# In the last pair of heads the rounded half of a probability is copied by VectorE instead of exponentiated a second time on ScalarE

## The chip, the cores and the metric

The kernel runs on one core of a Trainium2 chip. The metric is the device time of one launch in microseconds (us); lower is better. Engines are written as in the profile: PE is TensorE, ACT is ScalarE, DVE is VectorE, POOL is GpSimd, SP is SyncE, whose queue issues the DMAs here.

## The reference

One step of a one-layer streaming encoder: an RMS norm, one input projection that feeds two groups of attention heads, an output projection, and a SwiGLU feed-forward layer. The change lies in group A, the forgetting attention: 8 heads of 64, causal, over 1024 prompt rows and over 32 sample rows with 256 cached ones. Cut to it:

```python
s = jnp.einsum('bqhd,bkhd->bhqk', qi, k).astype(jnp.float32) * ATTN_SCALE
s = s + (ci[..., None] - cT[:, :, None, :])      # running sums of log forget gates
s = jnp.where((kpos[None, :] <= qpos[:, None])[None, None], s, NEG_INF)
p = jax.nn.softmax(s, axis=-1)
return jnp.einsum('bhqk,bkhd->bqhd', p.astype(v.dtype), v)
...
h = h + mixed @ w_out                            # both groups, each RMS-normalised
```

All data is float32.

## The kernel before, in words

**Split products.** PE multiplies a rounded 32-bit type (fp32r) fast, and the kernel keeps float32 accuracy by splitting every operand x into a rounded first half (hi) and the rest (lo = x - hi). A product is three matmuls, hi*hi, hi*lo and lo*hi (lines L526 to L528 for most of them, L719 for scores). So every operand costs two evictions or copies besides its computation.

**Units.** The heads are worked in four pairs. A pair has 15 units, numbered v = 15*pair + j, v from 0 to 59; the last pair is v = 45 to 59. A unit is one block of 128 keys against up to 512 queries, for both heads h of the pair. Queries go in three chunks: j = 0 to 3 have 512, 384, 256 and 128 queries, j = 4 to 8 have 512, j = 9 to 11 have 384, 256 and 128, and j = 12 to 14 are the sample's 32 rows. For each unit:

- `fox_scores(v)`: PE writes the scores of both heads to two banks of PSUM (six matmuls L719, on masked units some L725, last two L731). In the last pair it has two sets of banks and waits only for the exponentials of v-2.
- `fox_exp(v)`: ACT takes the exponential of each head's scores twice, once into `ph_x` in fp32r (the hi half, L1129) and once into `sp_x` in float32 (L1130). The second raises the semaphore `x_e`.
- `fox_lo(v)`: POOL waits for `x_e` and writes `pl_x = sp_x - ph_x` (L1834), one instruction a head, and raises `x_pl`.
- `fox_values(v)`: PE waits for `x_pl` of both heads and adds six matmuls (L526 to L528) to the output banks; it raises `x_pv`. The buffers of `ph_x` and `sp_x` go by v % 2, so `fox_exp(v)` waits for `x_pv` of v-2.

**The order.** Each engine has one program, written out step by step. PE in step v does `fox_scores(v)`, then the minima, projections and small transposes that a schedule gives to this step, then `fox_values(v-1)`. So scores run one unit ahead of values. What else is in the last pair:

- The output weights. In steps v = 46 to 53 ACT ends its step with `out_weights_hi` (`wo_hi`, L963, 128x1024) and DVE ends its own with `split_lo` (`wo_lo = raw - wo_hi`, L1352, both inputs in SBUF).
- The end of a chunk. ACT copies the output banks to `ot_x` (`fox_out`, L1144), PE transposes them (L612), and DVE divides them by their row sums (reciprocal L1454, product `og_x` L1458), from where a DMA stores them. For chunk 0 this is in step 50, where PE has these transposes, one of a small tile (`amx`, L599) and then `fox_values(49)`.
- The minima. In steps 45 to 48 DVE finishes the row minima of this pair (L1510), and POOL splits them into `tm_x` (L1845, L1847).
- The hand-over. In step 59 ACT (behind `fox_exp(59)`) and DVE (at the start of its step) do `groups_norm(0)`, the norm of the first 128 rows of mixed heads (squares L1210, a square root L1213 with the load of its table, DVE L1365, L1369 and twice L1609). In step 60 ACT has `fox_out(59)`, in step 61 PE and DVE have chunk 2's transposes and divisions. PE then waits until all of these are done before it transposes the normed rows (`turn_mixed(0)`, L846) and goes on to the output projection and the feed-forward layer.

Of the kernel before, what the change touches and what calls it, by code (L numbers as in the profile page):

```python
# [10 lines left out]
ACT = mybir.ActivationFunctionType  # L11
# [12 lines left out]
PAIRS = NH // 2  # L24
# [65 lines left out]
FU = make_fox()  # L90
# [222 lines left out]
def build(nc, x_p, x_s, ck_fox, cv_fox, cl_fox, ck_swa, cv_swa, rel_bias, g_attn, w_in, b_forget, sinks,  # L313
# [15 lines left out]
    with ExitStack() as ctx:  # L329
# [128 lines left out]
        def bank_view(b, m, start, *dims):  # L458
# [5 lines left out]
            f_mm f_ev f_t f_chain f_act f_bt f_c c_out c_in band_ps band_sb band_out band_in bias_ready  # L464
            st0 st1 st_misc
            w_s w_add w_e w_pl w_m w_ttr w_tm w_es w_pv w_ot w_den og_w0 og_w1
            x_s x_e x_pl x_m x_ttr x_tm x_pv x_ot x_den x_og ones
            o_in0 o_in1 o_in2 o_in3 o_in4 o_in5 o_in6 o_in7 o_in8
            c_xin0 c_xin1 c_sq1 c_ms1 c_rt1 c_ri1 c_xn1 c_t1 c_hi1 c_lo1 c_k c_op c_h2 c_sq2 c_ms2 c_rt2 c_ri2
            c_xn2 c_t2 c_t3 c_hi3 c_lo3  # L470
# [487 lines left out]
        def _(act):  # L958
# [161 lines left out]
            def fox_exp(v):  # L1120
                i, j = v // NFU, v % NFU
                _, vb, _, rows, _, n, _, _, _ = FU[j]
                if v >= 2:
                    act.wait_ge(S["x_pv"], 2 * (v - 1))
                b = score_bank(v)
                for h in range(2):
                    act.wait_ge(S["x_s"], 2 * v + h + 1)
                    decay = negc[0:rows, vb, 2 * i + h:2 * i + h + 1]
                    act.activation(ph_x[2 * (v % 2) + h][0:rows, 0:n], ps[0:rows, b + h, 0:n], ACT.Exp, bias=decay, scale=-1.0)  # L1129
                    act.activation(sp_x[2 * (v % 2) + h][0:rows, 0:n], ps[0:rows, b + h, 0:n], ACT.Exp, bias=decay, scale=-1.0)\  # L1130
                       .then_inc(S["x_e"], 1)

# [216 lines left out]
        def _(dve):  # L1349
# [143 lines left out]
            def fox_minima(i, g):  # L1493
# [9 lines left out]
                for h in range(2):  # L1503
# [4 lines left out]
                    if chained:  # L1508
                        dve.wait_ge(S["x_ttr"], 2 * (at - 1) + h + 1)
                    dve.tensor_tensor_reduce(s, s, cb[0:m, h, k0:k0 + nk], 1.0, part if chained else 3.0e38,  # L1510
                                             ALU.add, ALU.min, final if last else part).then_inc(S["x_ttr"], 1)

            def items(*place):

                for kind, a in plan(*place):
                    if kind == "task":
                        task(*a)
                    elif kind == "mw":
                        window_minima(*a)
# [93 lines left out]
            for v in range(-LEAD, NX + 2):  # L1613
                if v == NX - 1:
                    groups_norm(0)
                for part in range(5):
                    items("x", v, part)
                if 0 <= v - OUT_SPLITS < KB:
                    k = v - OUT_SPLITS
                    split_lo(SPLIT_OUT + k, raw2d[k % 3], wo_hi[:, k, :], wo_lo[:, k, :])  # L1620
# [111 lines left out]
        def _(pool):  # L1732
# [96 lines left out]
            def fox_lo(v):  # L1829
                _, _, _, rows, _, n, _, _, _ = FU[v % NFU]  # L1830
                for h in range(2):
                    pool.wait_ge(S["x_e"], 2 * v + h + 1)
                    at = 2 * (v % 2) + h
                    pool.tensor_tensor(pl_x[at][0:rows, 0:n], sp_x[at][0:rows, 0:n], ph_x[at][0:rows, 0:n].bitcast(F32),  # L1834
                                       ALU.subtract).then_inc(S["x_pl"], 1)
# [319 lines left out]
```

## Time and profile before

| | |
|---|---|
| median of 3 runs | 1499.74 us (1499.39 to 1500.48) |
| the profiled execution | 1497.76 us, span 1496.0 us |
| PE busy | 1410.3 us, 94% of the span |
| DVE, ACT, POOL busy | 579.4, 477.5 and 214.1 us |
| granted clock of PE, mean over the span | 0.976 |
| last pair, exponentials of v = 45 to 59 | 510.46 to 564.33 us from the span's start |

Times in rows are in us from the span's start. The table's shares are averages over stages with different limits; the last pair of heads is some 54 us of the span, and from 578 us on PE is busy without a gap. A row's "x2" merges two instructions that follow each other, its duration then reaches from the first's start to the second's end; what stands in brackets is the engine's idle time before it and what ended it.

### The profile page before, as it was taken

The numbers are of one execution on the slowest core, as the hardware profiler recorded it, in microseconds if no ns is written. First come the engines' busy times: TensorE is split into PE (matmuls) and PEld (weight loads), VectorE is DVE, ScalarE is ACT, GpSimd is POOL, SyncE is SP. The second block draws the span as 40 slices with busy tenths as digits, with TensorE's granted clock in tenths as the row PEclk, the third lists the DMA queues.
The fourth block names the chain that finished last, engine by engine and source line by source line (L and its number), as shares of the span: only waits on it lengthen the run. The fifth ranks groups of instructions, "written<-read, shape, count | busy, mean of one in ns | idle before, by whom it ended". The sixth has DMA issues, their size and how long they took to land.

```text
span 1496.0 us, 22497 instructions
## 1 busy us (share of the span) xinstructions
PE 1410.3 (94%) x9041; PEld 1303.2 (87%) x9041; DVE 579.4 (39%) x1374; ACT 477.5 (32%) x1044; POOL 214.1 (14%) x317
## 2 busy tenths in 40 slices
PE   5989987999999887999999999999999999999996
PEld 3878876877888756887999999999999999999996
DVE  6235542323232334444325242433333342425155
ACT  6336552354545473433321212021211112111103
POOL 2125542253524250000000000000000000000000
PEclk9999999999999898999999999999999999999998
DMA  7621113111212043112221111111111202020002
GB/s 193 111 60 30 34 44 98 44 47 41 90 41 73 23 135 124 43 40 64 85 79 38 54 43 43 43 43 43 43 43 42 61 25 71 15 73 30 12 1 116
DMA packets 104687, 87.34 MB, mean 58 GB/s; under 512 B 14336, under 2 KB 95328, under 8 KB 104072
## 3 DMA queue, kind: packets, MB, share of 16 engines
q1 hardware_dynamic: 104584, 85.91, 19.9%
q8 instruction: 72, 1.18, 0.3%
q14 instruction: 31, 0.25, 0.1%
HBM read 71.10 MB, written 14.89 MB: 57 GB/s over the span
## 4 chain that ended last, share of the span: by engine, by line
PE 87%; DVE 4%; ACT 3%; issue 3%; DMA 2%; POOL 1%; SPq 0%; DVEq 0%; ACTq 0%
PE ps L526 27%; PE ps L527 25%; PE ps L528 25%; PE ps L719 2%; PE ps L846 2%; DVE ps L1476 1%; PE ps L685 1%; DMA out<-outb 1%; PE ps L647 1%; DMA out<-raw 1%; PE ps L731 1%; PE ps L605 1%; ACT sp_x L1130 1%; ACT ph_x L1129 1%; DVE sp_w L1488 1%
## 5 line engine op out<-in xcount | busy, mean ns | idle before, releaser
L1682 DVE TENSOR_TENSOR outs<-outs,ps 128x384 f32<-128x384 f32 (+1 forms) x264 | 134.6, 510 | 108.7 <-PE ps L528 108.7
L1667 DVE TENSOR_TENSOR gu<-ps,sg 128x384 f32<-128x384 f32 (+1 forms) x66 | 34.6, 525 | 238.1 <-PE ps L528 238.1
L1834 POOL TENSOR_TENSOR pl_x<-sp_x,ph_x 128x512 fp32r<-128x512 f32 (+5 forms) x120 | 102.2, 866 | 149.4 <-ACT sp_x L1130 147.8
L1295 ACT ACTIVATE h_hi<-gu 128x384 fp32r<-128x384 f32 (+1 forms) x66 | 32.9, 498 | 222.7 <-DVE gu L1667 222.7
L1129 ACT ACTIVATE ph_x<-ps,negc 128x512 fp32r<-128x512 f32 (+5 forms) x120 | 63.1, 526 | 83.9 <-PE ps L731 83.9
L526 PE MATMUL ps<-f_hi,ff0hi 128*128 128x384 f32 (+1 forms) x264 | 85.7, 325 | 0.0
L526 PE MATMUL ps<-f_hi,ff3hi 128*128 128x384 f32 (+1 forms) x264 | 85.6, 324 | 0.0
L526 PE MATMUL ps<-f_hi,ff1hi 128*128 128x384 f32 (+1 forms) x264 | 85.6, 324 | 0.0
L526 PE MATMUL ps<-f_hi,ff2hi 128*128 128x384 f32 (+1 forms) x264 | 85.6, 324 | 0.0
L1289 ACT ACTIVATE sg<-ps 128x384 f32<-128x384 f32 (+1 forms) x66 | 30.5, 465 | 171.7 <-PE ps L528 171.7
L527 PE MATMUL ps<-f_lo,ff0hi 128*128 128x384 f32 (+1 forms) x264 | 85.2, 323 | 0.0
L527 PE MATMUL ps<-f_lo,ff1hi 128*128 128x384 f32 (+1 forms) x264 | 85.2, 323 | 0.0
L527 PE MATMUL ps<-f_lo,ff2hi 128*128 128x384 f32 (+1 forms) x264 | 85.2, 323 | 0.0
L527 PE MATMUL ps<-f_lo,ff3hi 128*128 128x384 f32 (+1 forms) x264 | 85.2, 323 | 0.0
L528 PE MATMUL ps<-f_hi,ff0lo 128*128 128x384 f32 (+1 forms) x264 | 85.1, 322 | 0.0
L528 PE MATMUL ps<-f_hi,ff1lo 128*128 128x384 f32 (+1 forms) x264 | 85.1, 322 | 0.0
L528 PE MATMUL ps<-f_hi,ff2lo 128*128 128x384 f32 (+1 forms) x264 | 85.1, 322 | 0.0
L528 PE MATMUL ps<-f_hi,ff3lo 128*128 128x384 f32 (+1 forms) x264 | 85.1, 322 | 0.0
L526 PE MATMUL ps<-h_hi,ff4hi 128*128 128x384 f32 (+1 forms) x240 | 82.1, 342 | 0.6 <-DVE outs L1686 0.5
L526 PE MATMUL ps<-h_hi,ff5hi 128*128 128x384 f32 (+1 forms) x240 | 78.3, 326 | 0.0
L527 PE MATMUL ps<-h_lo,ff5hi 128*128 128x384 f32 (+1 forms) x240 | 77.5, 323 | 0.0
L527 PE MATMUL ps<-h_lo,ff4hi 128*128 128x384 f32 (+1 forms) x240 | 77.4, 322 | 0.0
(290 smaller groups left out, 3799.5 us busy)
## 6 DMA issues: line engine op xcount, KB each, us to landing
raw<-in_w_gate SPq DMA_DIRECT2D x22, 512.0 KB, 5.2
raw<-in_w_up SPq DMA_DIRECT2D x22, 512.0 KB, 5.0
raw<-in_w_down SPq DMA_DIRECT2D x22, 512.0 KB, 4.0
raw<-in_w_in SPq DMA_DIRECT2D x14, 512.0 KB, 3.9
cb<-c_scratch SPq DMA_DIRECT2D x4, 1312.0 KB, 6.6
xt<-in_x_prompt SPq DMA_DIRECT2D x8, 512.0 KB, 4.3
out<-outb SPq DMA_DIRECT2D x16, 256.0 KB, 2.4
raw<-in_w_out SPq DMA_DIRECT2D x8, 512.0 KB, 3.5
```

The costliest lines, as they stand in the source:

```text
L526: pe.matmul(out, wh, xh, start=start, stop=False)
L527: pe.matmul(out, wh, xl, start=False, stop=False)
L528: return pe.matmul(out, wl, xh, start=False, stop=stop)
L605: mm = pe.transpose(ps[0:m, b, (2 * kv + x) * P:(2 * kv + x + 1) * P], ot_w[kv][:, x * m:(x + 1) * m], ident[:])
L719: pe.matmul(ps[0:rows, b + h, 0:n], keys[i % 2][hs, k0:k0 + rows], queries[i % 2][hs, q], start=(part == 0), stop=False)
L846: mm = pe.transpose(ps[:, banks[j], k * m:(k + 1) * m], src[0:m, (4 * j + k) * P:(4 * j + k + 1) * P], ident[0:m, 0:m])
L1129: act.activation(ph_x[2 * (v % 2) + h][0:rows, 0:n], ps[0:rows, b + h, 0:n], ACT.Exp, bias=decay, scale=-1.0)
L1289: act.activation(sg[c][:, 0:n], bank(c, n), ACT.Silu).then_inc(S["g_sg"], 1)
L1295: act.activation(h_hi[par][:, f, c0:c0 + n], gu[(f + c) % 2][:, 0:n], ACT.Copy).then_inc(S["g_hi"], 1)
L1667: dve.tensor_tensor(gu[(f + c) % 2][:, 0:n], bank(3 + c, n), sg[c][:, 0:n], ALU.mult)\
L1682: add = dve.tensor_tensor(y, y, bank(6 + o % 2, whole * P).rearrange("p (t m) -> p t m", t=whole), ALU.add)
L1834: pool.tensor_tensor(pl_x[at][0:rows, 0:n], sp_x[at][0:rows, 0:n], ph_x[at][0:rows, 0:n].bitcast(F32), ALU.subtract).then_inc(S["x_pl"], 1)
```

## The change

In the last pair (i = 3, v = 45 to 59) ACT makes one exponential a head, into `sp_x`. DVE copies it to `ph_x`, which rounds it, in a new function `fox_round(v)`, behind part 1 of its step v. POOL's `fox_lo(v)` waits there for the copies (`x_r`) instead of the exponentials. `fox_round(v)` waits for the same `x_pv` as `fox_exp(v)`. PE's and SP's programs stay as they are.

```diff
                 for h in range(2):
                     act.wait_ge(S["x_s"], 2 * v + h + 1)
                     decay = negc[0:rows, vb, 2 * i + h:2 * i + h + 1]
-                    act.activation(ph_x[2 * (v % 2) + h][0:rows, 0:n], ps[0:rows, b + h, 0:n], ACT.Exp, bias=decay, scale=-1.0)
+                    if i < PAIRS - 1:
+                        act.activation(ph_x[2 * (v % 2) + h][0:rows, 0:n], ps[0:rows, b + h, 0:n], ACT.Exp, bias=decay, scale=-1.0)
                     act.activation(sp_x[2 * (v % 2) + h][0:rows, 0:n], ps[0:rows, b + h, 0:n], ACT.Exp, bias=decay, scale=-1.0)\
                        .then_inc(S["x_e"], 1)
...
+            def fox_round(v):
+
+                _, _, _, rows, _, n, _, _, _ = FU[v % NFU]
+                dve.wait_ge(S["x_pv"], 2 * (v - 1))
+                for h in range(2):
+                    at = 2 * (v % 2) + h
+                    dve.wait_ge(S["x_e"], 2 * v + h + 1)
+                    dve.tensor_copy(ph_x[at][0:rows, 0:n], sp_x[at][0:rows, 0:n]).then_inc(S["x_r"], 1)
...
                 for part in range(5):
                     items("x", v, part)
+                    if part == 1 and NX - NFU <= v < NX:
+                        fox_round(v)
                 if 0 <= v - OUT_SPLITS < KB:
                     k = v - OUT_SPLITS
                     split_lo(SPLIT_OUT + k, raw2d[k % 3], wo_hi[:, k, :], wo_lo[:, k, :])
...
                 for h in range(2):
-                    pool.wait_ge(S["x_e"], 2 * v + h + 1)
+                    if v < NX - NFU:
+                        pool.wait_ge(S["x_e"], 2 * v + h + 1)
+                    else:
+                        pool.wait_ge(S["x_r"], 2 * (v - NX + NFU) + h + 1)
                     at = 2 * (v % 2) + h
                     pool.tensor_tensor(pl_x[at][0:rows, 0:n], sp_x[at][0:rows, 0:n], ph_x[at][0:rows, 0:n].bitcast(F32),
                                        ALU.subtract).then_inc(S["x_pl"], 1)
```

Below, lines of the changed kernel are one higher on ACT and up to ten higher on DVE than the same lines before. DVE's program in steps 48 to 52 was this before: the weights' lower halves of the steps 48 and 49, in step 50 the two divisions of chunk 0, and a weight's half in each of the steps 50, 51 and 52.

```order
L1352 TENSOR_TENSOR wo_lo<-raw_62,wo_hi 128x1024
L1352 TENSOR_TENSOR wo_lo<-raw_60,wo_hi 128x1024
L1454 RECIPROCAL small<-ps 128x4
L1458 TENSOR_TENSOR og_x<-ps,small 128x4x64
L1454 RECIPROCAL small<-ps 128x4
L1458 TENSOR_TENSOR og_x<-ps,small 128x4x64
L1352 TENSOR_TENSOR wo_lo<-raw_61,wo_hi 128x1024
L1352 TENSOR_TENSOR wo_lo<-raw_62,wo_hi 128x1024
L1352 TENSOR_TENSOR wo_lo<-raw_60,wo_hi 128x1024
```

Of the changed kernel the same place, up to the copies of step 51:

```order
L1353 TENSOR_TENSOR wo_lo<-raw_62,wo_hi 128x1024
L1521 CAST ph_x_101<-sp_x_156 128x512
L1521 CAST ph_x_158<-sp_x_157 128x512
L1353 TENSOR_TENSOR wo_lo<-raw_60,wo_hi 128x1024
L1521 CAST ph_x_99<-sp_x_154 128x512
L1521 CAST ph_x_100<-sp_x_155 128x512
L1455 RECIPROCAL small<-ps 128x4
L1459 TENSOR_TENSOR og_x<-ps,small 128x4x64
L1455 RECIPROCAL small<-ps 128x4
L1459 TENSOR_TENSOR og_x<-ps,small 128x4x64
L1353 TENSOR_TENSOR wo_lo<-raw_61,wo_hi 128x1024
L1521 CAST ph_x_101<-sp_x_156 128x512
```

Two copies (`ph_x_101` and `ph_x_158` for odd units, `ph_x_99` and `ph_x_100` for even ones) now stand between any two weight halves, and in step 50 ahead of the divisions.

The end of DVE's last pair was this before: the divisions of chunk 1, `groups_norm(0)`, and the divisions of chunk 2.

```order
L1454 RECIPROCAL small<-ps 128x4
L1458 TENSOR_TENSOR og_x<-ps,small 128x4x64
L1365 TENSOR_SCALAR small<-small 128x2
L1369 RECIPROCAL small<-small 128x2
L1609 SCALAR_TENSOR_TENSOR raw_61<-oq,small,gains 128x512 x2
L1454 RECIPROCAL small<-ps 32x1
L1458 TENSOR_TENSOR og_x<-ps,small 32x64
```

Of the changed kernel the same place:

```order
L1455 RECIPROCAL small<-ps 128x4
L1459 TENSOR_TENSOR og_x<-ps,small 128x4x64
L1366 TENSOR_SCALAR small<-small 128x2
L1370 RECIPROCAL small<-small 128x2
L1619 SCALAR_TENSOR_TENSOR raw_61<-oq,small,gains 128x512 x2
L1521 CAST ph_x_101<-sp_x_156 32x32
L1521 CAST ph_x_158<-sp_x_157 32x32
L1455 RECIPROCAL small<-ps 32x1
L1459 TENSOR_TENSOR og_x<-ps,small 32x64
```

The copies of unit 59 stand behind the whole of `groups_norm(0)`, since DVE does that at the start of step 59.

ACT's program in steps 51 and 52 was this before, one unit of four exponentials and a weight's upper half, and the start of the next:

```order
L1129 ACTIVATE ph_x_101<-ps,negc 128x512
L1130 ACTIVATE sp_x_156<-ps,negc 128x512
L1129 ACTIVATE ph_x_158<-ps,negc 128x512
L1130 ACTIVATE sp_x_157<-ps,negc 128x512
L963 ACTIVATE wo_hi<-raw_62 128x1024
L1129 ACTIVATE ph_x_99<-ps,negc 128x512
```

and is this in the changed kernel:

```order
L1131 ACTIVATE sp_x_156<-ps,negc 128x512
L1131 ACTIVATE sp_x_157<-ps,negc 128x512
L963 ACTIVATE wo_hi<-raw_62 128x1024
L1131 ACTIVATE sp_x_154<-ps,negc 128x512
L1131 ACTIVATE sp_x_155<-ps,negc 128x512
```

Each unit has two instructions fewer in front of its weight's upper half.

## Rows read from the trace of the kernel before

**Rows 1.** Busy time by stretch: bounds, length, then PE, PEld, DVE, ACT, POOL, clock, DMA.

```profile
531.00:539.00 8.00, 4.57 (x32) 3.19 (x29) 3.58 (x6) 8.00 (x15) 4.01 (x4) 1.00 0.36 114
539.00:554.00 15.00, 12.86 (x67) 7.99 (x66) 6.14 (x4) 12.03 (x20) 9.19 (x8) 0.89 0.64 224
578.00:704.00 126.00, 126.00 (x662) 103.61 (x661) 60.29 (x109) 48.22 (x115) 0.00 (x0) 0.99 0.16 51
```

**Rows 2.** Timeline of PE in steps 51 to 54: values (L526) and scores (L719).

```profile
540.07 0.79 PE L719 MATMUL ps<-q_hi,k_hi 64*128 64x512 f32 x2
...
546.15 0.50 PE L526 MATMUL ps<-ph_x,vw_hi 128*128 128x512 f32 x1 [0.85 <-POOL pl_x L1834]
...
547.74 0.50 PE L719 MATMUL ps<-q_hi,k_hi 64*128 64x512 f32 x2
...
549.62 0.50 PE L526 MATMUL ps<-ph_x,vw_hi 128*128 128x512 f32 x1 [0.50 <-POOL pl_x L1834]
...
553.14 0.50 PE L526 MATMUL ps<-ph_x,vw_hi 128*128 128x512 f32 x1 [0.78 <-POOL pl_x L1834]
```

**Rows 3.** Timeline of ACT in the same steps.

```profile
542.24 0.69 ACT L1129 ACTIVATE ph_x<-ps,negc 128x512 fp32r<-128x512 f32 x1 [2.63 <-PE ps L731]
...
544.53 1.07 ACT L963 ACTIVATE wo_hi<-raw 128x1024 fp32r<-128x1024 f32 x1
...
549.21 0.69 ACT L1129 ACTIVATE ph_x<-ps,negc 128x512 fp32r<-128x512 f32 x1 [0.35 <-PE ps L731]
```

**Rows 4.** Timeline of POOL, units 49, 51, 52 and, first head alone, 54.

```profile
533.26 2.50 POOL L1834 TENSOR_TENSOR pl_x<-sp_x,ph_x 128x512 fp32r<-128x512 f32 x2 [2.31 <-ACT sp_x L1130]
...
543.58 2.52 POOL L1834 TENSOR_TENSOR pl_x<-sp_x,ph_x 128x512 fp32r<-128x512 f32 x2 [3.56 <-ACT sp_x L1130]
546.84 2.73 POOL L1834 TENSOR_TENSOR pl_x<-sp_x,ph_x 128x512 fp32r<-128x512 f32 x2 [0.74 <-ACT sp_x L1130]
...
553.61 1.44 POOL L1834 TENSOR_TENSOR pl_x<-sp_x,ph_x 128x384 fp32r<-128x384 f32 x1 [0.52 <-ACT sp_x L1130]
```

**Rows 5.** Timeline of DVE: three of the eight lower halves of output weights.

```profile
545.64 1.54 DVE L1352 TENSOR_TENSOR wo_lo<-raw,wo_hi 128x1024 fp32r<-128x1024 f32 x1 [4.54 <-ACT wo_hi L963]
548.90 1.75 DVE L1352 TENSOR_TENSOR wo_lo<-raw,wo_hi 128x1024 fp32r<-128x1024 f32 x1 [1.72 <-ACT wo_hi L963]
552.61 1.56 DVE L1352 TENSOR_TENSOR wo_lo<-raw,wo_hi 128x1024 fp32r<-128x1024 f32 x1 [1.97 <-ACT wo_hi L963]
```

**Rows 6.** Timeline of DVE: the instructions nearest to the new copy.

```profile
514.07 0.69 DVE L1416 TENSOR_TENSOR vw_lo<-ps,vw_hi 128x512 fp32r<-128x512 f32 x1 [2.15 <-ACT vw_hi L1079]
...
565.73 0.17 DVE L1365 TENSOR_SCALAR small<-small 128x2 f32<-128x2 f32 x1 [2.36 <-ACT raw L1210]
```

**Rows 7.** Timeline of DVE and PE around step 50, the end of chunk 0.

```profile
536.29 1.23 DVE L1352 TENSOR_TENSOR wo_lo<-raw,wo_hi 128x1024 fp32r<-128x1024 f32 x1 [3.00 <-ACT wo_hi L963]
...
538.12 0.24 PE L599 MATMUL ps<-ident,tm_x 32*128 32x32 f32 x1 [2.04 <-DVE og_x L1458]
```

**Rows 8.** Timeline of all engines over steps 59 to 61 and the hand-over.

```profile
563.54 0.28 ACT L1129 ACTIVATE ph_x<-ps,negc 32x32 fp32r<-32x32 f32 x1 [1.18 <-PE ps L731]
...
564.07 0.58 POOL L1834 TENSOR_TENSOR pl_x<-sp_x,ph_x 32x32 fp32r<-32x32 f32 x2 [1.38 <-ACT sp_x L1130]
...
564.71 0.28 PE L526 MATMUL ps<-ph_x,vw_hi 32*128 32x32 f32 x1 [0.49 <-POOL pl_x L1834]
...
565.28 0.26 PE L528 MATMUL ps<-ph_x,vw_lo 32*128 32x32 f32 x1
...
567.12 0.27 ACT L1144 ACTIVATE ot_x<-ps 128x32 f32<-128x32 f32 x2
...
567.44 1.42 DVE L1609 SCALAR_TENSOR_TENSOR raw<-oq,small,gains 128x512 f32<-128x512 f32 x2
...
569.46 0.21 DVE L1458 TENSOR_TENSOR og_x<-ps,small 32x64 f32<-32x64 f32 x1
569.99 1.94 PE L846 MATMUL ps<-ident,raw 128*128 128x128 f32 x8 [1.96 <-DVE og_x L1458]
```

More of the change, by code:

```diff
@@ L466, in build @@
             w_s w_add w_e w_pl w_m w_ttr w_tm w_es w_pv w_ot w_den og_w0 og_w1
-            x_s x_e x_pl x_m x_ttr x_tm x_pv x_ot x_den x_og ones
+            x_s x_e x_pl x_m x_ttr x_tm x_pv x_ot x_den x_og x_r ones
             o_in0 o_in1 o_in2 o_in3 o_in4 o_in5 o_in6 o_in7 o_in8
```

## Prediction

> **What bounds the kernel now.** I read the busy time by stretch first. From 578 us on PE has no gap [rows 1], so whatever delays the hand-over at the end of the last pair stays in the total. Inside the pair it is not so: of 531 to 539 us PE works 4.57 of 8.00 while ACT is busy for all of it, and of 539 to 554 PE works 12.86 of 15.00. Then I read PE's timeline for what ends those gaps. Each `fox_values` starts on POOL's `pl_x` after 0.50 to 0.85 us of waiting [rows 2]. So in the large units the bound is a loop through four engines. For unit 51, ACT starts at 542.24 [rows 3], POOL 1.34 later, at 543.58, and runs 2.52, to 546.10 [rows 4]; PE starts values(51) at 546.15. They last until scores(53) at 547.74, 1.59 later [rows 2], and ACT starts unit 53 at 549.21, 1.47 after that [rows 3]. Sum of the loop: 3.91 + 1.59 + 1.47 = 6.97 us, and values(51) to values(53) is 6.99. It carries every second unit, so a unit takes 3.5 us. Only what lengthens 3.91 counts, and half of it for each unit.
>
> **What the trace shows of DVE against POOL.** A weight's lower half takes 1.23 us alone, at 536.29 [rows 7]. The one asked at 545.64 ends at 547.18, 1.08 after POOL's 546.10. The one asked at 548.90 ends at 550.65, 1.08 after POOL's end at 546.84 + 2.73 = 549.57. It works the other way round as well: POOL begins the first head of unit 54 at 553.61 and ends it at 555.05, while DVE holds on to 552.61 + 1.56 = 554.17; the 0.88 behind that is all that 384 elements need [rows 4, 5]. So a DVE instruction with two inputs in SBUF and a POOL instruction exclude each other, and the later one waits in full. Before the change this is nearly free: `wo_lo` is asked when ACT's `wo_hi` ends, 544.53 + 1.07, near the end of POOL's second head, and it clears out before POOL's next unit, but for some 0.2 to 0.5. The Trainium skill, page "SBUF — State Buffer", section "Who interferes with whom", states this as a rule: the two share a port pair under an exclusive lock, whichever issued first. By that rule, the trace agrees, to the 1.08.
>
> **The change part by part.** ACT loses two exponentials a unit, 0.57 each in the large units (544.53 - 542.24 = 2.29 for four [rows 3]). DVE gains two copies. The trace has no copy from SBUF to SBUF on DVE. Its bounds are 0.17 (an instruction on two elements) and 0.69 (512 elements at one a cycle, from PSUM and SBUF [rows 6]); I take 0.69, the row with the copy's own size, and show what the other end does. The Trainium skill, page "VectorE: DVE Perf Modes", section "The perf-mode tier table", gives fp32 copies within SBUF twice that rate, an estimate of 0.42 for 512; its SBUF page adds that such a copy takes the port pair too.
>
> *Step a, the chain of a large unit (51).* From T, ACT's start. Now: first exponential, 0.69 and a hand-over of 0.08, then copy 0.69 and 0.08, so POOL starts at T + 1.54 in place of T + 1.34. Its first head ends at T + 2.79. By then the second copy is done, but ACT's `wo_hi` ends at T + 1.14 + 1.07 = T + 2.2, so DVE asks for `wo_lo` at about T + 2.3, in the middle of POOL's first head, no longer at the end of its second. It is next: T + 2.79 to T + 3.87. POOL's second head follows, to T + 5.12, and values start at T + 5.2. That is 1.3 more than 3.91. If POOL keeps its turn for the second head, `wo_lo` runs from T + 4.04 to T + 5.12, the next unit's first copy, wanted at T + 3.5 + 0.77 = T + 4.27, waits 0.85, and the loss is about 1.0 instead. With a copy of 0.42 that also excludes POOL, the second copy can't run under POOL's first head; it and `wo_lo` go between the heads (0.30 + 1.13 after POOL's first head at T + 1.27 to T + 2.52), and the end is again at T + 5.2. The three orders agree within 0.3.
>
> *Step b, units 52 and 53.* Now the turn-taking itself sets the pace: one copy 0.69 (nothing of this unit runs beside it), POOL 1.25, `wo_lo` 1.08, POOL 1.25, and some 0.15 of hand-overs, 4.4 us a unit against 3.5. Two units, 2 x 0.9 = 1.8. With the short copy the sum is 0.30 + 1.25 + 0.30 + 1.13 + 1.25 + 0.15, the same 4.4. Units 54 to 58 have no weights behind them; there a copy replaces an exponential in the chain, within 0.1 each either way, taken as 0.
>
> *Step c, step 50.* Before, DVE does its `wo_lo` at 536.29, then the divisions, and PE starts the small transpose at 538.12, with values(49) right behind it [rows 7]. The two copies of unit 50 now stand ahead of the divisions: 2 x 0.69 = 1.4. POOL's unit 49, which began at 533.26 [rows 4], starts behind its copies some 1.1 later, so its second head ends near where `wo_lo` begins, or after it: 1.1 more for one of them. Against it ACT, which never rests here [rows 1], reaches `wo_hi` 2 x 0.57 = 1.1 earlier. Sum +1.4; bounds 0.3 (short copies) and 2.0 (all of it in a row).
>
> *Step d, steps 45 to 48.* Their units are small or their weight halves far from POOL's work; PE waits there for evictions and minima. ACT's saved 1.1 at unit 45 advances the first eviction by about 0.3, and the copies in step 47 push POOL's `tm_x` back by more than that. This is inside the bounds of step c, which was counted from the present times.
>
> *Step e, the hand-over.* In E, ACT's start of unit 59, 563.54 before. ACT begins the squares 0.34 earlier, so `groups_norm(0)` ends on DVE at 567.44 + 1.42 - 0.34, E + 4.98 [rows 8]. Only then come the copies of unit 59, whose values so far ran under the load of the table. Now in a row: copy 0.17, POOL 0.08 + 0.58, PE 0.06 + 0.83 (564.71 to 565.54), ACT 0.1 + 0.27, transposes 0.3, divisions of the second head 0.4, and 0.3 to the start of L846 (569.67 to 569.99). E + 4.98 + 3.1 = E + 8.1; before it was E + 6.45. That is +1.6, and with PE's small matmuls slower after a rest of 4 us I take +1.9 (1.6 to 2.4). No work covers it: all engines wait for the same chain. SP's stores and loads behind `x_pv` and `og_x` shift with it and keep their lead over PE.
>
> **Sum.** 1.3 + 1.8 + 1.4 + 1.9 = 6.4 us. The profiled execution took 1497.76, which gives 1504.2; the median lies 1.98 above it, so I forecast 1499.74 + 6.4 = 1506.1. Bounds: 0.7 + 1.2 + 0.3 + 1.6 = 3.8 and 1.5 + 2.2 + 2.0 + 2.4 = 8.1, so 1503.5 to 1507.8 in this case.
>
> **Rivals.** *The copies slip between.* If POOL's two heads stay together and `wo_lo` ends before the next copy is due, steps a to c come to nothing, since a copy takes the place of an exponential of about its own length; step e stays. 1499.74 + 1.9 = 1501.6. Against it: `wo_lo` and both heads need 1.08 + 2.5, more than the 3.5 of a unit, already. *The clock falls.* PE's rests grow from 0.5 to 0.85 to some 1.5 us a unit. In 539 to 554 us the mean granted clock is 0.89 [rows 1], and scores(51), at 540.07 after the gap of step 50, took 0.79 for their first two matmuls instead of 0.50 [rows 2]. At the lower level, 1.2 GHz, values and scores of a large unit take some 1.2 more; for two more units 2.5, so 1508.6. *ScalarE's relief decides* (the other side). ACT is busy for the whole of 531 to 539. If its queue is the bound there and in 542 to 552, where `wo_hi` ends just as the next unit is due, 1.1 are saved at each of two units and 0.3 at unit 45; with short copies another 0.15 for each of three units. That is 3.0 off, against 1.9 of step e: 1498.6. It decides over step a as soon as `wo_lo` costs POOL less than 0.3 a unit; to be faster by over 0.2% it would need 4.9 off.
>
> **How the numbers follow.** My forecast has 0.63, the clock 0.15, the slipping copies 0.15, ScalarE's relief 0.07. About 0.2%, 3.0 us, is what a measurement of this kernel can tell from no change. The forecast and the clock give slower, 0.78; I add 0.01 for mixtures. Both others lie within 3.0 us: 0.22, less 0.03 for a larger relief. So faster 0.03, same 0.18, slower 0.79. The range takes in the slipping copies' 1501.6 and the clock's 1508.6: 1501.4 to 1508.8.
>
> **What would show it.** `wo_lo` of steps 51 to 53 begins between POOL's two heads, which no longer follow each other without a gap. From ACT's start to PE's values, unit 51 takes 5.2 instead of 3.91, and values(51) to values(53) 8.7 instead of 6.99. L846 starts 8.1 to 8.9 after ACT's start of unit 59 instead of 6.45. I am wrong if POOL's heads stay together and the spacing stays at 7.0, or if the copies take under 0.3.

## The result and the profile after

The changed kernel takes 1506.86 us (median of 6 runs, 1504.33 to 1509.70), the kernel before 1500.11 us beside it (6 runs, 1498.55 to 1501.64). The ratio is 1.0045, 95% interval 1.0032 to 1.0058: slower by 6.75 us, where 6.4 was forecast.

| | before | after |
|---|---|---|
| the profiled execution | 1497.76 us, span 1496.0 | 1509.70 us, span 1507.9 |
| PE busy | 1410.3 us | 1416.0 us |
| DVE, ACT, POOL busy | 579.4, 477.5, 214.1 us | 591.5, 466.2, 217.8 us |
| mean granted clock | 0.976 | 0.966 |

The profiled execution is the slowest of its six and 11.9 us longer than the one of before. Of that, 3.77 us lie ahead of ACT's start of unit 45 (514.23 against 510.46), where the programs are equal (the mean clock of the first 100 us is 0.90 after and 0.97 before), and 0.3 behind the hand-over (from L846's start to the end it is 926.3 us after and 926.0 before). So the change is read between two marks, ACT's start of unit 45 and the start of L846: 67.35 us after, 59.53 before, 7.82 more. This is the timeline of all engines after, steps 49 to 53, as [rows 2] to [rows 5] and [rows 7] show them before (start, duration, engine, line, operation, what it waited for):

```profile
538.73 1.29 ACT L1131 ACTIVATE sp_x<-ps,negc 128x512 f32<-128x512 f32 x2
538.90 2.26 DVE L1353 TENSOR_TENSOR wo_lo<-raw,wo_hi 128x1024 fp32r<-128x1024 f32 x1 [1.18 <-ACT wo_hi L963]
541.09 0.75 DVE L1521 CAST ph_x<-sp_x 128x512 fp32r<-128x512 f32 x2
541.76 0.17 DVE L1455 RECIPROCAL small<-ps 128x4 f32<-128x4 f32 x1
...
542.44 0.31 PE L599 MATMUL ps<-ident,tm_x 32*128 32x32 f32 x1 [3.75 <-DVE og_x L1459]
542.68 0.80 PE L526 MATMUL ps<-ph_x,vw_hi 128*128 128x512 f32 x1
...
547.71 1.27 ACT L1131 ACTIVATE sp_x<-ps,negc 128x512 f32<-128x512 f32 x2 [3.78 <-PE ps L731]
548.50 2.08 DVE L1521 CAST ph_x<-sp_x 128x512 fp32r<-128x512 f32 x2 [3.21 <-ACT sp_x L1131]
548.87 1.06 ACT L963 ACTIVATE wo_hi<-raw 128x1024 fp32r<-128x1024 f32 x1
549.01 1.29 POOL L1849 TENSOR_TENSOR pl_x<-sp_x,ph_x 128x512 fp32r<-128x512 f32 x1 [4.80 <-DVE ph_x L1521]
550.51 1.21 DVE L1353 TENSOR_TENSOR wo_lo<-raw,wo_hi 128x1024 fp32r<-128x1024 f32 x1
550.66 2.18 POOL L1849 TENSOR_TENSOR pl_x<-sp_x,ph_x 128x512 fp32r<-128x512 f32 x1 [0.36 <-DVE ph_x L1521]
551.64 1.82 DVE L1521 CAST ph_x<-sp_x 128x512 fp32r<-128x512 f32 x2
552.90 0.50 PE L526 MATMUL ps<-ph_x,vw_hi 128*128 128x512 f32 x1 [2.27 <-POOL pl_x L1849]
553.21 3.61 POOL L1849 TENSOR_TENSOR pl_x<-sp_x,ph_x 128x512 fp32r<-128x512 f32 x2 [0.36 <-DVE ph_x L1521]
553.39 2.31 DVE L1353 TENSOR_TENSOR wo_lo<-raw,wo_hi 128x1024 fp32r<-128x1024 f32 x1
...
556.72 0.43 DVE L1521 CAST ph_x<-sp_x 128x512 fp32r<-128x512 f32 x1 [1.03 <-ACT sp_x L1131]
556.87 0.50 PE L526 MATMUL ps<-ph_x,vw_hi 128*128 128x512 f32 x1 [1.03 <-POOL pl_x L1849]
...
561.07 0.50 PE L526 MATMUL ps<-ph_x,vw_hi 128*128 128x512 f32 x1 [1.47 <-POOL pl_x L1849]
```

A copy of 512 takes 0.43 alone (556.72) and two in a row 0.75 (541.09), not 0.69 apiece. In unit 51, though, the pair takes 2.08 (548.50): the first ends before POOL starts, at 549.01, and the second ends only 0.28 after POOL's first head, 550.58 against 550.30. Then `wo_lo` (550.51) goes, and POOL's second head needs 2.18 instead of 1.25. This is the order that step a gave for the short copy, and values(51) start 5.19 after ACT (552.90 - 547.71). The Trainium skill, page "VectorE: DVE Perf Modes", section "The perf-mode tier table", gives such copies two elements a cycle, and its page "SBUF — State Buffer", section "Who interferes with whom", says that they take the port pair in that mode. The trace agrees with both, to the 0.43 and the 550.58.

The hand-over after, as [rows 8]:

```profile
572.87 0.45 ACT L1131 ACTIVATE sp_x<-ps,negc 32x32 f32<-32x32 f32 x2 [3.10 <-PE ps L731]
...
576.44 1.41 DVE L1619 SCALAR_TENSOR_TENSOR raw<-oq,small,gains 128x512 f32<-128x512 f32 x2
577.77 0.25 DVE L1521 CAST ph_x<-sp_x 32x32 fp32r<-32x32 f32 x2
578.01 0.45 POOL L1849 TENSOR_TENSOR pl_x<-sp_x,ph_x 32x32 fp32r<-32x32 f32 x2 [7.59 <-DVE ph_x L1521]
...
578.51 0.39 PE L526 MATMUL ps<-ph_x,vw_hi 32*128 32x32 f32 x1 [4.34 <-POOL pl_x L1849]
...
581.03 0.21 DVE L1459 TENSOR_TENSOR og_x<-ps,small 32x64 f32<-32x64 f32 x1
...
581.58 1.94 PE L846 MATMUL ps<-ident,raw 128*128 128x128 f32 x8 [0.86 <-DVE og_x L1459]
```

The norm ends on DVE, and only then come copy, POOL, PE, ACT and the divisions one after the other: 581.58 - 572.87 = 8.71, against 6.45. Last, the busy time by stretch after. The first two answer to [rows 1], the others are where the clock was low:

```profile
531.00:539.00 8.00, 5.66 (x40) 4.11 (x40) 4.24 (x11) 5.04 (x10) 4.85 (x10) 1.00 0.30 87
539.00:554.00 15.00, 9.29 (x34) 6.11 (x35) 10.70 (x14) 6.59 (x10) 7.97 (x6) 0.77 0.67 238
541.00:549.00 8.00, 6.56 (x20) 4.40 (x21) 3.71 (x9) 2.43 (x5) 2.62 (x2) 0.57 0.54 175
568.00:573.00 5.00, 5.00 (x39) 4.74 (x38) 1.80 (x8) 1.88 (x7) 0.93 (x4) 0.57 0.05 14
```

ACT is no longer full (5.04 of 8.00), and from 539 to 554 PE works 9.29 us instead of 12.86, at a mean clock of 0.77 instead of 0.89. Some of that is only the shift of 3.77 us: in the stretch that answers to it, 542.77 to 557.77, PE works 11.70 us at 0.82. The 7.82 us divide by marks of the two timelines:

| piece | before | after | more |
|---|---|---|---|
| ACT's unit 45 to values(49), step 50's divisions | 27.84 | 28.45 | 0.61 |
| values(49) to ACT's unit 51, PE alone | 3.94 | 5.03 | 1.09 |
| ACT's unit 51 to values(51) | 3.91 | 5.19 | 1.28 |
| values(51) to values(53) | 6.99 | 8.17 | 1.18 |
| values(53) to ACT's unit 59 | 10.40 | 11.80 | 1.40 |
| ACT's unit 59 to L846 | 6.45 | 8.71 | 2.26 |

Two of the pieces, 2.49 us together, are PE at its lower level: in the second PE works without a rest in both kernels, but after the change the mean clock from 541 to 549 is 0.57 and its matmuls mostly run at the lower level, 1.2 GHz (L526 at 542.68 takes 0.80). In the fifth the eight transposes L612 of chunk 1 took 1.97 instead of 1.12, here after the change and then before it:

```profile
569.15 1.97 PE L612 MATMUL ps<-ident,ot_x 128*128 128x128 f32 x8
```

```profile
561.30 1.12 PE L612 MATMUL ps<-ident,ot_x 128*128 128x128 f32 x8
```

This division is that of one execution. Where the clock falls is not the same each time, as a1 and a4 below show.

### The profile page after: what moved, and what is told of

Read it like the earlier page. It is cut to its first block, busy times and chain, and to the rows that moved or that the text cites. A ratio compares the mean times of both kernels' runs of the same rounds, so it can differ in the third digit from the quotient of the medians.

```text
span 1507.9 us, 22512 instructions
## 1 busy us (share of the span) xinstructions
PE 1416.0 (94%) x9041; PEld 1308.9 (87%) x9041; DVE 591.5 (39%) x1404; ACT 466.2 (31%) x1014; POOL 217.8 (14%) x317
## 3 DMA queue, kind: packets, MB, share of 16 engines
q8 instruction: 72, 1.18, 0.3%
## 4 chain that ended last, share of the span: by engine, by line
PE 88%; DVE 4%; issue 3%; ACT 2%; DMA 2%; POOL 1%; DVEq 0%; SPq 0%; POOLq 0%; ACTq 0%
PE ps L526 27%; PE ps L527 25%; PE ps L528 25%; PE ps L719 2%; PE ps L846 2%; DVE ps L1477 1%; PE ps L685 1%; DMA out<-outb 1%; PE ps L647 1%; PE ps L731 1%; DMA out<-raw 1%; PE ps L605 1%; POOL pl_x L1849 1%; DVE sp_w L1489 1%; ACT sp_x L1131 0%
## 5 line engine op out<-in xcount | busy, mean ns | idle before, releaser
L1849 POOL TENSOR_TENSOR pl_x<-sp_x,ph_x 128x512 fp32r<-128x512 f32 (+5 forms) x120 | 107.1, 906 | 156.3 <-ACT sp_x L1131 119.2
L526 PE MATMUL ps<-f_hi,ff0hi 128*128 128x384 f32 (+1 forms) x264 | 85.8, 325 | 0.0
L526 PE MATMUL ps<-f_hi,ff3hi 128*128 128x384 f32 (+1 forms) x264 | 85.7, 325 | 0.0
L526 PE MATMUL ps<-f_hi,ff1hi 128*128 128x384 f32 (+1 forms) x264 | 85.7, 325 | 0.0
L526 PE MATMUL ps<-f_hi,ff2hi 128*128 128x384 f32 (+1 forms) x264 | 85.7, 325 | 0.0
L526 PE MATMUL ps<-h_hi,ff4hi 128*128 128x384 f32 (+1 forms) x240 | 82.3, 343 | 0.6 <-DVE outs L1698 0.5
L526 PE MATMUL ps<-h_hi,ff5hi 128*128 128x384 f32 (+1 forms) x240 | 78.3, 326 | 0.0
L528 PE MATMUL ps<-h_hi,ff5lo 128*128 128x384 f32 (+1 forms) x240 | 77.4, 322 | 0.0
```

The source lines that it names most:

```text
L526: pe.matmul(out, wh, xh, start=start, stop=False)
L528: return pe.matmul(out, wl, xh, start=False, stop=stop)
```

## The experiments

Every kernel of the experiments was timed in 5 to 12 runs, beside 21 to 29 of the kernel before. "1", "2", "3" are the three lengths of its one profiled execution: ACT's start of unit 45 to that of unit 51, to that of unit 59, to L846. "Marks" is their sum less the 59.53 of before, "median" its median less that of the kernel before beside it. The ratio is not that of the medians (0.001 of it is 1.5 us): for d1, whose runs lie in two groups, it says 7.0 us, the median 10.43.

| kernel | 1 | 2 | 3 | marks | median | ratio (95%) |
|---|---|---|---|---|---|---|
| before | 31.78 | 21.30 | 6.45 | | | |
| the change | 33.48 | 25.16 | 8.71 | +7.82 | +6.75 | 1.0045 (1.0032, 1.0058) |
| a1, unit 59 ahead of the norm | 31.22 | 26.53 | 6.14 | +4.36 | +4.72 | 1.0036 (1.0024, 1.0049) |
| a2, `wo_lo` from one source | 30.68 | 21.53 | 8.68 | +1.36 | +1.48 | 1.0016 (1.0008, 1.0025) |
| a3, units 54 to 59 alone | 31.66 | 21.77 | 8.67 | +2.57 | +3.21 | 1.0025 (1.0016, 1.0034) |
| a4, units 45 to 58 alone | 31.03 | 26.49 | 6.45 | +4.44 | +5.91 | 1.0041 (1.0028, 1.0054) |
| c1, copy at one element a cycle | 33.21 | 24.89 | 8.69 | +7.26 | +6.54 | 1.0043 (1.0031, 1.0055) |
| c2, units 49 to 53 alone | 32.75 | 25.10 | 6.45 | +4.77 | +4.82 | 1.0032 (1.0019, 1.0046) |
| d4, units 51 to 53 alone | 31.70 | 26.23 | 6.45 | +4.85 | +4.79 | 1.0024 (1.0014, 1.0034) |
| d1, unit 50's copies behind the divisions | 32.61 | 26.23 | 8.68 | +7.99 | +10.43 | 1.0047 (1.0029, 1.0065) |
| b1, POOL's part on DVE, two exponentials | 34.37 | 19.72 | 6.45 | +1.01 | +1.94 | 1.0011 (1.0002, 1.0020) |
| b2, POOL's part on DVE, one exponential | 33.23 | 19.75 | 6.14 | -0.41 | -0.07 | 1.0001 (0.9992, 1.0009) |
| d3, b1 with d1's order | 32.09 | 19.72 | 6.44 | -1.28 | -0.12 | 0.9996 (0.9986, 1.0006) |
| d2, b2 with d1's order | 31.15 | 19.76 | 6.10 | -2.52 | -3.88 | 0.9973 (0.9961, 0.9985) |

Up to unit 58 the change, a1 and a4 are the same program, and still lengths 1 and 2 are 33.48 and 25.16, 31.22 and 26.53, 31.03 and 26.49. In the change's profile the lower clock lies in step 50 and ahead of unit 59, in the other two between values(51) and values(53) (9.70 and 9.65 us apart, against 8.17) and behind values(53). So a single length can move by 2.4 us with the place where the clock falls, while the sum of the two is 5.56, 4.67 and 4.44 over the 53.08 of before. All seven kernels in which `wo_lo` stands between POOL's heads (the change, a1, a4, c1, c2, d4, d1) have such a stretch at the lower level in length 2, and 24.89 us or more for it. The kernel before and the six others (a2, a3, b1, b2, d2, d3) have none there, and 21.77 or less.

**a1: the hand-over.** The changed kernel with the copies of unit 59 ahead of `groups_norm(0)`.

```diff
                 if v == NX - 1:
+                    fox_round(v)
                     groups_norm(0)
...
-                    if part == 1 and NX - NFU <= v < NX:
+                    if part == 1 and NX - NFU <= v < NX - 1:
```

> The changed kernel with one move: VectorE copies unit 59 ahead of groups_norm(0) instead of behind it. Theory (the hand-over costs what the order says): from ScalarE's start of unit 59 to the first transpose L846 it falls from 8.71 us to 6.5 or less (6.45 before the change), and the kernel is some 2.2 us faster than the changed one, about 4.6 us over the kernel before. Rival (VectorE's order is not the cause, the clock or the port is): it stays above 8.

The hand-over falls from 8.71 to 6.14, and the kernel stands 4.72 over that of before instead of 6.75, as expected. So step e's cost is the place of two copies of 32 elements behind the norm, and all of it goes away with that.

**a2: the weight's lower half off the port.** Here `wo_lo` is computed from `raw` alone, times zero, with an accumulator: one input, one element a cycle. It leaves the lower halves of the output weights out of the result.

```diff
-                    split_lo(SPLIT_OUT + k, raw2d[k % 3], wo_hi[:, k, :], wo_lo[:, k, :])
+                    dve.wait_ge(S["cw_hi"], SPLIT_OUT + k + 1)
+                    dve.tensor_scalar(wo_lo[:, k, :], raw2d[k % 3], 0.0, 0.0, ALU.mult, ALU.add,
+                                      accum_out=small[:, 206 + k:207 + k]).then_inc(S["cw_lo"], 1)
```

> The changed kernel with VectorE's eight weight halves replaced by an instruction with one SBUF source and an accumulator, of the same 1024 elements (the lower half of w_out is left out of the computation: it is written as zeros). Theory (the port): VectorE is as busy as before, but POOL's second head no longer waits for the weight half; unit 51 takes 4.2 us from ScalarE's start to TensorE's values instead of 5.2, values(51) to values(53) 7.2 to 7.5 instead of 8.2, and the kernel is 2.5 to 3.5 us faster than the changed one. Rival (VectorE's queue alone: its instructions stand in each other's way, no port): the intervals stay at 5.2 and 8.2, the time at that of the changed kernel.

The timeline of its units 51 and 52:

```profile
544.72 1.27 ACT L1131 ACTIVATE sp_x<-ps,negc 128x512 f32<-128x512 f32 x2 [2.98 <-PE ps L731]
...
546.02 2.80 POOL L1851 TENSOR_TENSOR pl_x<-sp_x,ph_x 128x512 fp32r<-128x512 f32 x2 [3.93 <-DVE ph_x L1521]
546.97 1.22 DVE L1633 TENSOR_SCALAR_CACHE_REDUCE wo_lo<-raw 128x1024 fp32r<-128x1024 f32 x1 [0.52 <-ACT wo_hi L963]
...
548.88 0.50 PE L526 MATMUL ps<-ph_x,vw_hi 128*128 128x512 f32 x1 [1.41 <-POOL pl_x L1851]
```

`wo_lo` takes its 1.22 beside POOL, whose two heads stay together in 2.80 (3.6 to 3.8 in the changed kernel). Values(51) start 4.16 after ACT, values(53) 7.19 after values(51), and lengths 1 and 2 are 0.87 under those of before. What is left of the loss is the hand-over. The kernel is 5.3 us under the change by the medians, where 2.5 to 3.5 was expected: the expectation counted the turn-taking alone, and by the profile the falls of the clock in length 2 are gone too. The turn-taking between `wo_lo` and POOL thus carries all of the large units' loss, the clock's part with it.

**a3 and a4: the change in two parts.** a3 has it in units 54 to 59 alone, a4 in 45 to 58. Only the bounds of v in the three places of the diff differ.

> The change for units 54 to 59 alone, where no output weight is split; units 45 to 53 are as before the change. Theory (port and order): only the hand-over is dearer, so 1.9 to 2.3 us over the kernel before. Rival (each copy costs its own length plus a hand-over): six units at 0.3 more each on top, 3.5 to 4 us over it. Rival (the clock): if TensorE's clock falls near 568 us as in the changed kernel, 1.4 more.

> The change for units 45 to 58; unit 59 is as before the change, with two exponentials a head. Theory: the hand-over is back at 6.45 us, the slow stretch with the weight halves stays, 4.2 to 4.8 us over the kernel before. Rival (the slow stretch is the clock's): it varies by the clock alone and is under 2.5 over it when the clock in 539 to 554 us is that of before, 0.89.

In a3 length 2 grows by 0.47 and the hand-over by 2.22. Its median, 3.21 over, lies above the 1.9 to 2.3 expected and below the rival's 3.5 to 4; the marks, 2.57, with 0.47 for units 54 to 58 together instead of the rival's 0.3 for each of six, side with the first. In a4 length 2 grows by 5.19 and the hand-over not at all. It is 5.91 over by the median, more than the 4.2 to 4.8 expected, and 4.44 by the marks. Its rival fails: the clock from 539 to 554 is 0.89, that of before, and it is far more than 2.5 over. The medians of the two, 3.21 and 5.91, come to 9.1, more than the whole change's 6.75; the marks, 2.57 and 4.44, come to 7.01 of 7.82.

**c1: the copy itself off the port.** The copy is a multiplication by 1 with an accumulator, which goes to an unused column of `small` (`spare(v, h)`, a new function not shown).

```diff
-                    dve.tensor_copy(ph_x[at][0:rows, 0:n], sp_x[at][0:rows, 0:n]).then_inc(S["x_r"], 1)
+                    dve.tensor_scalar(ph_x[at][0:rows, 0:n], sp_x[at][0:rows, 0:n], 1.0, 0.0, ALU.mult, ALU.add,
+                                      accum_out=small[0:rows, spare(v, h):spare(v, h) + 1]).then_inc(S["x_r"], 1)
```

> The changed kernel, with its copies written as a multiplication by 1 with an accumulator, which goes one element a cycle and has one input; nothing is left out. If it does not exclude POOL, the second copy of a unit takes about 0.6 to 0.69 beside POOL's first head instead of waiting 1.1 for it. Theory (the lower half of the weight is what separates POOL's heads, the second copy only joins it): the orders agree within 0.3 a unit, so ACT's start to values of unit 51 stays 5.0 to 5.4, values(51) to values(53) 8.0 to 8.7, and the time is that of the changed kernel within 1.5 us. Rival (it is the second copy's wait for the port that delays the unit): values(51) to values(53) falls by 1 or more, and the time by 2 to 3 us.

```profile
544.25 0.68 DVE L1525 TENSOR_SCALAR_CACHE_REDUCE ph_x<-sp_x 128x512 fp32r<-128x512 f32 x1
544.41 6.96 POOL L1854 TENSOR_TENSOR pl_x<-sp_x,ph_x 128x512 fp32r<-128x512 f32 x4 [4.78 <-DVE ph_x L1525]
...
545.08 1.70 DVE L1353 TENSOR_TENSOR wo_lo<-raw,wo_hi 128x1024 fp32r<-128x1024 f32 x1
```

In this timeline the second copy runs its 0.68 beside POOL's first head instead of waiting for it, and nothing is gained: values(51) start 5.14 after ACT, and the median is that of the change, +6.54. The second copy only joins a gap that `wo_lo` makes anyway. Values(51) to values(53), expected up to 8.7, was 9.49, and the clock fell in it: L526 of values(52) takes 0.68 (see d4).

**c2 and d4: the large units alone.** c2 has the change in units 49 to 53, d4 in 51 to 53.

> The change for units 49 to 53 alone, the large ones with weight halves behind them; the ten others keep their two exponentials; nothing is left out. Theory: steps a, b and c of the change are all here, and the hand-over is not: the hand-over is 6.4 to 6.5, ACT's start of unit 45 to its start of unit 59 is 56.5 to 58 instead of 53.1, and the time is 3.5 to 4.5 us over that of before. Rival (the copies of all units add up, each costing about the same): five of fifteen units, so 1.5 to 2 us over that of before.

> The change for units 51, 52 and 53 alone; nothing is left out. Steps a and b of the prediction are here, c and e not: 3.1 us over that of before by the prediction (2.5 to 3.5 by the changed kernel's trace, 1.3 for the chain of unit 51 and 1.2 between values(51) and values(53)), hand-over 6.4 to 6.5, ACT's start of unit 45 to unit 51 as before, 31.5 to 32.2. Against the kernel with units 49 to 53 (4.8 over that of before) the difference is step c, 1.3 to 2.0. Rival (the clock makes most of it): ACT's start of unit 51 to that of unit 59 grows by 4 or more, from 21.3 to over 25.

c2 is 4.82 over that of before, a little more than the 3.5 to 4.5 expected and far from its rival's 1.5 to 2; its hand-over, 6.45, and its other mark, 57.85, are as expected. d4 is not: it costs 4.79 instead of 3.1, and the mark that its rival named, length 2 over 25, is at 26.23. Timeline of its PE:

```profile
547.02 0.39 PE L731 MATMUL ps<-am_x,minus 64*128 64x512 f32 x2
549.93 0.49 PE L526 MATMUL ps<-ph_x,vw_hi 128*128 128x512 f32 x1 [2.52 <-POOL pl_x L1849]
...
550.53 0.63 PE L528 MATMUL ps<-ph_x,vw_lo 128*128 128x512 f32 x1
...
559.63 0.50 PE L526 MATMUL ps<-ph_x,vw_hi 128*128 128x512 f32 x1 [2.54 <-POOL pl_x L1849]
```

and its busy time by stretch:

```profile
547.00:550.00 3.00, 0.48 (x5) 0.07 (x1) 2.95 (x2) 2.23 (x4) 2.88 (x2) 1.00 1.00 325
550.00:554.00 4.00, 4.00 (x18) 2.42 (x18) 2.71 (x3) 0.00 (x0) 3.61 (x2) 0.57 0.59 242
554.00:559.00 5.00, 3.09 (x24) 1.88 (x20) 2.56 (x3) 4.03 (x7) 3.20 (x2) 1.00 0.00 0
560.00:564.00 4.00, 4.00 (x21) 2.89 (x20) 0.00 (x0) 0.71 (x2) 1.51 (x2) 0.58 0.00 0
```

Two units start close together (ACT at 544.80 and 547.51), PE then rests 2.52 us in one piece, and 0.6 us into the next work its granted clock falls from full to half (2.4 to 1.2 GHz) for some 3.4 us: a matmul of `fox_values` goes from 0.39 to 0.63. The same again after the rest of 2.54, 1.0 us into the work. Values(51) to values(53) is 9.70 here against 8.17 in the change's profile, 1.5 more. With the seven kernels named under the table this says that the turn-taking also costs through the clock. That a rest of some length brings the fall is not shown: the change's own rest of 2.27 before 552.90 is followed by full speed, and one of 2.04 in the kernel before ([rows 7]) by the lower level at 540.07. And c2 minus d4 is no measure of step c.

**d1: step 50 alone.** The changed kernel with unit 50's copies behind the divisions of step 50.

```diff
-                    if part == 1 and NX - NFU <= v < NX:
+                    if part == (3 if v == NX - 10 else 1) and NX - NFU <= v < NX:
```

> The changed kernel, with the two copies of unit 50 behind the divisions of step 50 instead of ahead of them; nothing is left out. Step c of the prediction: the copies, 0.75 together in the changed kernel, stand in the divisions' way, while the other part, the weight's lower half that waits 1.05 for POOL, stays. So the transposes behind the divisions start 0.7 to 0.8 earlier against ACT's start of unit 45, and the time is 0.5 to 1.0 us under the changed kernel's, which this measurement can hardly tell. Rival (unit 50's copies, now later, hold up its own values): the time is that of the changed kernel or over it.

Step 50's transpose (L599) starts 3.04 after ACT's start of unit 50 (541.88 - 538.84), in the changed kernel 3.71: the 0.67 is there. Against ACT's start of unit 45, the mark that was named, it is only 0.17 earlier (28.04 for 28.21), since unit 50 itself starts 0.50 later in this execution, ahead of anything that the edit moves. The time did not follow. Length 1 is 0.87 under the change's, but 1.4 over that of a1 and a4; length 2 is 1.07 over (rests of 2.19 and 2.56 us, each followed by the lower clock), and the median is 10.43 over that of before. The ratio's interval, 4.3 to 9.7 us, takes in that of the change, so no gain or loss of d1 against it is shown. Its runs lie in two groups, 1503.84 and 1504.67 at mean clocks of 0.974 and 0.973, and four from 1509.31 to 1510.00 at 0.967 and 0.968. The six of the change run the same way from 1504.33 at 0.974 to 1509.70 at 0.966. Which group a run falls in outweighs 0.67 us; what decides it is open.

**b1 and b2: POOL out of the loop.** In the last pair DVE does the subtraction too, unit 59 ahead of the norm. b1 keeps both exponentials and copies nothing, b2 has one exponential and the copy; d2 and d3 are these with unit 50's instructions behind the divisions. Of b2:

```diff
+                    dve.tensor_copy(ph_x[at][0:rows, 0:n], sp_x[at][0:rows, 0:n]).then_inc(S["x_c"], 1)
+                    dve.wait_ge(S["x_c"], 2 * (v - NX + NFU) + h + 1)
+                    dve.tensor_tensor(pl_x[at][0:rows, 0:n], sp_x[at][0:rows, 0:n], ph_x[at][0:rows, 0:n].bitcast(F32),
+                                      ALU.subtract).then_inc(S["x_r"], 1)
```

> The kernel before, ScalarE still writes both exponentials, but in the last pair VectorE does the subtraction for the lower half instead of POOL (unit 59's ahead of the group norm); nothing is left out. Port theory: with POOL out of it no VectorE instruction waits for the port. Two subtractions of 512 with two inputs in SBUF take at most 0.69 each, against 2.52 for POOL's two, so for unit 51 ACT's start to PE's values is about 3.2 instead of 3.91, values(51) to values(53) about 6.3 instead of 6.99, hand-over near 6.1 to 6.5; the whole 1.5 to 3.5 us faster than before. Rival (VectorE's queue is the bound, not the exclusion by POOL): the two subtractions push the weights' lower halves and the divisions back, values(51) to values(53) stays at 7 or more, and the time is that of before or 1 to 2 us over it.

> The changed kernel (one exponential, copy on VectorE), but in the last pair VectorE also does the subtraction, so that POOL has no part in a unit; unit 59's copies and subtractions stand ahead of the group norm; nothing is left out. Port theory: the copies themselves cost little (0.38 apiece), what cost the change its time was POOL and VectorE taking turns. Then for unit 51 ACT's start to PE's values is 2.9 to 3.3 instead of the change's 5.2, values(51) to values(53) 6.0 to 6.6 instead of 8.2, hand-over 6.1 to 6.5, the whole 2 to 4 us faster than before, that is 8 to 10 under the changed kernel. Rival (the copies load VectorE's queue, whoever subtracts): four instructions a unit there, 8.2 stays at 7.5 or more, and the time is not under that of before.

The loops were near what was expected: values(51) to values(53) 6.53 in b2 (547.56 to 554.09) and 6.53 in b1, and length 2 is 1.55 and 1.58 under that of before. The totals were not: 0.07 under and 1.94 over, where 2 to 4 and 1.5 to 3.5 under were expected. Those are the totals that the rivals named, though not by their loop of 7 us or more. The next two kernels show what was left out, step c. Timeline of b1 around step 50:

```profile
541.52 0.69 DVE L1522 TENSOR_TENSOR pl_x<-sp_x,ph_x 128x512 fp32r<-128x512 f32 x1
...
542.68 0.69 DVE L1522 TENSOR_TENSOR pl_x<-sp_x,ph_x 128x512 fp32r<-128x512 f32 x1 [0.46 <-ACT sp_x L1133]
543.29 0.17 DVE L1457 RECIPROCAL small<-ps 128x4 f32<-128x4 f32 x1
...
543.98 0.31 PE L599 MATMUL ps<-ident,tm_x 32*128 32x32 f32 x1 [3.82 <-DVE og_x L1461]
```

The divisions stand behind two subtractions that wait for ACT's exponentials, and length 1 is 2.59 over that of before, some of it PE's lower level again (values(49), at 544.22, take 0.79 for the first matmul); in b2 it is 1.45. Hence the last two:

> As the kernel in which VectorE does one copy and the subtraction and POOL nothing (it took the time of before), with unit 50's four instructions behind the divisions of step 50; nothing is left out. Theory: that kernel is quicker by 1.55 us from unit 51 to unit 59 and loses 1.45 before unit 51, because unit 50's four instructions (2.1 us) stand ahead of the divisions. Then ACT's start of unit 45 to that of unit 51 is 31.2 to 32.0 us instead of 33.2, and the time is 1.2 to 2.2 us under that of before, a ratio of 0.9985 to 0.9992. Rival (the 1.45 is the clock, or unit 50's own chain, and not the divisions): no change against that kernel, the time of before.

> As the kernel with two exponentials on ScalarE and the subtraction on VectorE (1.9 us over that of before), with unit 50's two subtractions behind the divisions of step 50; nothing is left out. Theory: there VectorE waited in order for unit 50's exponentials (subtractions at 541.52 and 542.68) with the divisions behind, and PE rested 3.82 us for them. Then ACT's start of unit 45 to that of unit 51 falls from 34.4 to 31.5 to 32.2 us, and the time is 2 to 3 us under that kernel's, 0 to 1.2 under that of before. Rival: no change against that kernel.

d2 is faster than both kernels, 1495.20 us (12 runs), ratio 0.9973. Its timeline in unit 51 to 53:

```profile
545.85 1.27 ACT L1134 ACTIVATE sp_x<-ps,negc 128x512 f32<-128x512 f32 x2 [3.14 <-PE ps L731]
...
546.63 0.43 DVE L1524 CAST ph_x<-sp_x 128x512 fp32r<-128x512 f32 x1 [1.41 <-ACT sp_x L1134]
...
547.10 0.69 DVE L1526 TENSOR_TENSOR pl_x<-sp_x,ph_x 128x512 fp32r<-128x512 f32 x1
...
548.77 1.22 DVE L1356 TENSOR_TENSOR wo_lo<-raw,wo_hi 128x1024 fp32r<-128x1024 f32 x1
548.91 0.50 PE L526 MATMUL ps<-ph_x,vw_hi 128*128 128x512 f32 x1 [0.45 <-DVE pl_x L1526]
...
552.17 0.50 PE L526 MATMUL ps<-ph_x,vw_hi 128*128 128x512 f32 x1 [0.30 <-DVE pl_x L1526]
```

DVE does copy, subtraction, copy, subtraction and `wo_lo` without a gap, 3.26 us a unit, and values start 3.06 after ACT. Length 1 fell from 33.23 to 31.15, as expected. The time, 3.88 us under that of before, is more than the 1.2 to 2.2 expected and 1.4 more than the marks; that is not explained. d3 has the same order with two exponentials. It gained 2.28 of length 1 against b1 (34.37 to 32.09) and 2.1 of median, but ends at the time of before, where its marks stand 1.28 under it; its interval allows either. By the marks, then, half of d2's 2.52 us is there with both exponentials, from taking POOL out; the other half, 0.94 of it in length 1 and 0.34 in the hand-over, comes with the second exponential that ACT no longer makes.

## Why the prediction was right

The forecast was right in its sign, its size (6.4 for 6.75) and the place of the loss, but not in every term.

- **Steps a and b, the port.** Shown. The chain of unit 51 took 5.19 for 5.2. The pace was sized high: values(51) to values(53) 8.17 instead of 8.7, POOL's units following at 4.20 and 4.02 instead of 4.4, so 2.46 for 3.1. a2 shows that `wo_lo` against POOL makes it, c1 that the copy's own use of the port does not, b2 and d2 that without POOL the loop is 0.46 shorter than before (6.53 for 6.99). It is the order in this pair that is shown; a kernel that keeps POOL and only puts `wo_lo` behind its second head was not run.
- **The copy's cost.** 0.69 was taken and 0.38 to 0.43 measured. The sum did not hang on it, since both orders end at T + 5.2; the one seen is the short copy's.
- **Step c.** Oversized: 0.61 for 1.4 (0.50 in a1 and 0.31 in a4, the same program there). The copies in the divisions' way cost 0.67 (d1), and `wo_lo` waits for POOL's unit 49 there, 2.26 instead of 1.23. But it is asked for 1.16 earlier too (24.67 after ACT's unit 45 instead of 25.83), since ACT is done with the upper half sooner. That cancels the longer wait, and the copies remain.
- **Step e.** Right: 2.26 for 1.9 (1.6 to 2.4), with the chain as written. a1 undoes it whole.
- **Units 54 to 58.** Put at 0, they cost 0.5 alone (a3), and in the change's profile nothing beside the clock: of the fifth piece's 1.40, 1.48 lie between L612 and ACT's unit 59 (569.15 to 572.87 against 561.30 to 563.54), where PE works without a rest in both and only the clock differs.
- **What the sum left out: the clock.** It stood beside the forecast as a rival, 2.5 us more, and it came true beside it: 2.49 us of the change's profile, and two stretches of some 3.4 us in d4. Its size was taken from too small a price: values and scores of a large unit took 4.87 us together at the lower level (542.68 to 547.55), against 1.59 and 1.20 at the full one, so 2.1 more for one unit and not 1.2. In the change's profile the lower level met one large unit and the small ones ahead of unit 59. With a, b, c and e at their measured sizes the sum is 5.33, and the clock's 2.49 makes it 7.82. By the marks the rival's total would be the nearer one; by the median, 6.75, the forecast is. That it came out within 0.4 us is in part luck: step c and the pace were 1.4 us too large together, where the clock, 2.5, was left out.
- **ScalarE's relief.** No gain: ACT falls to 5.04 of 8.00, and PE waits more, not less. The relief is real only where it isn't followed by POOL and DVE on one port: in a2 lengths 1 and 2 are 0.87 under those of before, and in d2 0.90 under those of d3, which keeps both exponentials and is itself 1.27 under those of before.

## What to carry to other kernels

Before work is moved from a busy engine to an idle one, ask what it does to the order in which DVE and POOL want the port: here the idle time of DVE and the copy's length were both fine, and what cost 2.5 us, and some more through the clock, was that the weight's lower half was asked for 1.1 us earlier in its unit, between two instructions of POOL instead of behind them. Moving the whole of such a chain to one engine, so that nobody takes turns, was worth more than spreading it. And an instruction added to an in-order queue is paid by what stands behind it: look for the divisions or the norm there first, since two copies of 32 elements behind the wrong neighbour cost 2.3 us.

## What the runs showed of the hardware

- A DVE instruction that waits for the port gets it between two instructions of POOL that are both ready: `wo_lo`, asked at 553.39 in POOL's first head, ends at 555.70, and POOL's pair of heads stretches to 3.61, although the copy for its second head was done by 553.46.
- One input, one element a cycle and an accumulator: such DVE instructions ran beside POOL at full speed, 0.68 for 512 elements (c1) and 1.22 for 1024 (a2). The SBUF page of the Trainium skill, in the section cited above, names this form as one that stays off the pair.
- A rest of PE of 2.5 us in one piece was followed, 0.6 to 1.0 us into the next work, by some 3.4 us at the lower clock (d4, twice). The length of the rest alone does not decide it: after 2.27 us in the change (to 552.90) and 2.37 in c1 (to 557.46) the clock stayed full, after 2.04 in the kernel before it fell. In d2, whose rests there are 0.3 to 0.5, values(51), (52) and (53) follow each other at 3.26 at full speed.
